# Attention and feed-forward in one block, narrow decode down products, and the last two groups finished row by row

## What is computed

```python
def hybrid_layer(x, ...):
    h = rmsnorm(x, norm_mix_pre)
    rq, rk, rv, rg, dq, dk, dv = split(h @ w_in)
    ret_out = silu(rg) * rms_normalize(retention(rope(rq), rope(rk), rv))
    diff_out = rms_normalize(diff_attention(rope(dq), rope(dk), dv))
    x = x + rmsnorm(concat(ret_out, diff_out) @ w_out, norm_mix_post)
    u = rmsnorm(x, norm_ffn_pre) @ w_up
    f = square(relu(u)) @ w_down
    return x + rmsnorm(f, norm_ffn_post)
```

## Time and profile before

| | us |
|---|---|
| median of 3 runs | 3050.96 (3050.58 to 3054.31) |
| the profiled execution | 3052.13 |
| its span, first to last instruction | 3050.3 |
| PE busy | 2894.8 |
| DVE busy | 1497.1 |
| ACT busy | 927.0 |
| POOL busy | 286.8 |

### The profile page before, as it was taken

The page is one execution under the profiler, slowest core; times in us unless marked ns, Lnnn a source line. Parts: engine busy times, 40 slices in busy tenths (PEclk is TensorE's granted clock), DMA queues, the critical chain, the costliest instruction groups (busy, mean ns, idle before and its releaser), DMA issues.

```text
span 3050.3 us, 39356 instructions
## 1 busy us (share of the span) xinstructions
PE 2894.8 (95%) x14977; PEld 2383.3 (78%) x14977; DVE 1497.1 (49%) x3014; ACT 927.0 (30%) x1852; POOL 286.8 (9%) x420
## 2 busy tenths in 40 slices
PE   6999997999969999999699999999989999999996
PEld 5888885778857777777478888888878989899895
DVE  4332233333247877777444444444565444544446
ACT  3222223222136666666321211121142112121112
POOL 1111220111111111100000000000021000000003
PEclk9999998999979999999799999999999999999998
DMA  4101103333332211110411111111042111111112
GB/s 161 34 27 32 35 21 130 126 100 124 125 124 83 68 65 56 39 43 29 147 60 42 54 42 51 46 41 55 28 141 96 42 41 41 45 51 41 41 55 100
DMA packets 105888, 204.68 MB, mean 67 GB/s; under 512 B 11248, under 2 KB 48112, under 8 KB 105776
## 3 DMA queue, kind: packets, MB, share of 16 engines
q1 hardware_dynamic: 103472, 194.79, 19.4%
q0 software_dynamic: 2304, 8.39, 0.8%
HBM read 168.28 MB, written 34.87 MB: 67 GB/s over the span
## 4 chain that ended last, share of the span: by engine, by line
PE 48%; DVE 2%; DMA 0%; ACT 0%; issue 0%; SPq 0%
PE bank L2135 24%; PE bank L2099 24%; DVE ffn_facc L1933 1%; PE bank L2090 0%; DVE ffn_upl L1907 0%; DVE ffn_facc L1974 0%; DVE ffn_hTl L1926 0%; DVE ffn_x L1920 0%; DMA ffn_gain_x<-in_norm_ffn_pre_dram 0%; DMA ffn_raw<-in_w_up_dram 0%; DVE ffn_dnl L1914 0%; DMA ffn_x<-x_scratch 0%; ACT ffn_hTh L1796 0%; ACT ffn_relu L1816 0%; DVE ffn_facc L1940 0%
## 5 line engine op out<-in xcount | busy, mean ns | idle before, releaser
L1974 DVE TENSOR_TENSOR ffn_facc<-bank,ffn_facc 128x512 f32<-128x512 f32 x510 | 345.9, 688 | 243.8 <-PE bank L2135 242.6
L2099 PE MATMUL bank<-ffn_hTh,ffn_uph 128*128 128x352 f32 (+1 forms) x1280 | 451.0, 352 | 8.7 <-DVE ffn_upl L1907 5.5
L2099 PE MATMUL bank<-ffn_hTl,ffn_uph 128*128 128x352 f32 (+1 forms) x1280 | 449.6, 351 | 0.0
L2099 PE MATMUL bank<-ffn_hTh,ffn_upl 128*128 128x352 f32 (+1 forms) x1280 | 449.4, 351 | 0.0
L2135 PE MATMUL bank<-ffn_dnh,ffn_hidh 128*128 128x512 f32 x1088 | 430.6, 396 | 9.4 <-DVE ffn_dnl L1914 6.2
L2135 PE MATMUL bank<-ffn_dnh,ffn_hidl 128*128 128x512 f32 x1088 | 430.7, 396 | 0.0
L2135 PE MATMUL bank<-ffn_dnl,ffn_hidh 128*128 128x512 f32 x1088 | 429.8, 395 | 0.0
L1947 DVE SCALAR_TENSOR_TENSOR ffn_relu<-bank,ffn_relu 128x352 f32<-128x352 f32 (+1 forms) x160 | 94.5, 591 | 482.2 <-ACT ffn_relu L1816 482.0
L2099 PEld LDWEIGHTS bank<-ffn_hTh,ffn_uph 128*128 128x128 f32 x1280 | 241.1, 188 | 33.7 <-issue 7.7
L2099 PEld LDWEIGHTS bank<-ffn_hTl,ffn_uph 128*128 128x128 f32 x1280 | 241.3, 188 | 23.6
L2099 PEld LDWEIGHTS bank<-ffn_hTh,ffn_upl 128*128 128x128 f32 x1280 | 241.1, 188 | 22.6
(11 more groups left out here) (196 smaller groups left out, 4393.3 us busy)
## 6 DMA issues: line engine op xcount, KB each, us to landing
ffn_raw<-in_w_up_dram SPq DMA_DIRECT2D x64, 512.0 KB, 4.5
ffn_raw<-in_w_down_dram SPq DMA_DIRECT2D x64, 512.0 KB, 4.1
ffn_x<-x_scratch SPq DMA_DIRECT2D x24, 512.0 KB, 4.1
retp_x<-in_x_prompt_dram SPq DMA_DIRECT2D x16, 512.0 KB, 3.6
retw_raw<-in_w_in_dram SPq DMA_DIRECT2D x16, 512.0 KB, 5.0
dpp_x<-in_x_prompt_dram SPq DMA_DIRECT2D x16, 512.0 KB, 5.0
dp_kst<-in_cache_diff_k_dram SPq DMA_DIRECT2D x32, 256.0 KB, 2.8
mix_xr<-in_x_prompt_dram SPq DMA_DIRECT2D x16, 512.0 KB, 3.4
```

The lines of the kernel that those rows point to most:

```text
L1974: nc.vector.tensor_tensor(out=part, in0=Dn[i % s.rd][:], in1=part, op=ALU.add).then_inc(s_add, 1)
L2099: last = nc.tensor.matmul(bank[:, 0:w], l[:, k, f * P:(f + 1) * P], r[:, k, c:c + w], start=(k == 0 and q == 0), stop=(k == 7 and q == 2))
```

## The change

Retention start: ACT takes the mean square of row tile 1 after eight of the 16 weight pieces. The constants are loaded between and behind the weight pieces: the small table behind piece 7, decay behind piece 11, the second rope table and the decode state behind piece 15.

Joined stages: attention and feed-forward are one phase, without a barrier between them. The programs of the attention are generators that yield at named points, and the feed-forward's programs run their first steps there. The feed-forward's buffers take the place of those of the attention that are free by then. On DVE the split of the last mixed rows now comes before the normalisation of tile 15.

Narrow decode products: ACT keeps a fp32 copy of the 32 decode columns of each hidden unit (`hd`). `decode_down` multiplies it with the unrounded weights in `raw`, as four fp32 matmuls with a 128x32 stationary tile, each into its own 32 rows of the bank `DD`, summed there over all 16 groups. `decode_sum` adds the two partial sums of each half with a matrix `pick`. The second block then has 96 matmuls per group and four banks in turn instead of three.

Last two groups: their second products are taken together, 12 matmuls into one bank, with the weights of the last group in the buffers of the up weights, and one accumulation for both. POOL makes only the inverse roots there; DVE multiplies with the gain while the root is made and finishes a row with one instruction. All residual rows have buffers of their own, seven of them loaded ahead.

```diff
                 wt.load(sp, wv, 0, slice(0, 4))
                 sp.dma_start(rope[0][:], rv[0][:, 0:192]).then_inc(s_rope[0], 16)
                 pre.load(sp, xv[1], 1)
-                sp.dma_start(rope[1][:], rv[1][:, 0:192]).then_inc(s_rope[1], 16)
-                sp.dma_start(decay[:], ret_tab[:, 0:4 * P]).then_inc(s_const, 16)
+                wt.load(sp, wv, 0, slice(4, 8))
                 sp.dma_start(small[:], ret_tab[:, 4 * P:4 * P + 12]).then_inc(s_const, 16)
+                wt.load(sp, wv, 0, slice(8, 12))
+                sp.dma_start(decay[:], ret_tab[:, 0:4 * P]).then_inc(s_const, 16)
+                wt.load(sp, wv, 0, slice(12, 16))
+                sp.dma_start(rope[1][:], rv[1][:, 0:192]).then_inc(s_rope[1], 16)
                 sp.dma_start(state[1][:].rearrange("d (h v) -> d h v", h=4),
                              state_in.rearrange("h d v -> d h v")).then_inc(s_const, 16)
-                wt.load(sp, wv, 0, slice(4, None))
...
-                wt.act_hi(act)
+                wt.act_hi(act, slice(0, 8))
+                pre.act_meansq(act, 1, 1, 2)
+                wt.act_hi(act, slice(8, 16))
...
+        def decode_down(g, e):
+            count = 2 * G + 2 * g + 3 - (1 if isinstance(g, int) and g == G - 1 else 0)
+            pe.wait_ge(s_hd, FG * (g + 1))
+            for i in range(FG):
+                pe.wait_ge(s_raw[i], 16 * count)
+            for n in range(2):
+                for f in range(FG):
+                    rows_out = slice((FG * n + f) * dec, (FG * n + f + 1) * dec)
+                    last = nc.tensor.matmul(DD[rows_out, :], hd[e][:, f, :], raw[f][:, n * N:(n + 1) * N],
+                                            start=(isinstance(g, int) and g == 0),
+                                            stop=(isinstance(g, int) and g == G - 1))
+            last.then_inc(s_dq, 1)
...
+        def down_both(s):
...
+            for i in range(s.rd):
+                half(i, 0)
+            decode_down(G - 1, 1)
+            pe.wait_ge(s_wlo, 8 * G)
+            pe.wait_ge(s_hl, s.u0 + G * s.ku)
+            for i in range(s.rd):
+                half(i, 1).then_inc(s_d, 1)
+            for i in range(s.rd, s.kd):
+                pe.wait_ge(s_add, 4 + d0 + i + 1 - s.rd)
+                half(i, 0)
+                if i == s.rd:
+                    decode_sum()
+                half(i, 1).then_inc(s_d, 1)
...
+                next(mixing)
+                pe.wait_ge(before_it.s_sc, before_it.read_pairs)
+                x_transpose(0)
+                x_transpose(1)
+                next(mixing)
+                x_transpose(2)
+                x_transpose(3)
+                next(mixing, None)
                 first_up(s, 0, range(0, 4))
...
+                if s.b and not last:
+                    sp.wait_ge(s_dq, g + 1)
...
                 hid_lo(s, 0, 0, 0, fu)
+                next(mixing, None)
...
                 x_lo(6)
...
+        for p, i in enumerate(s.order):
+            if i in s.whole:
+                accumulate(s, G - 2, i)
+            else:
+                decode_row()
+            if p:
+                last_row(p - 1)
+            gained(p)
+        last_row(s.nb - 1)
```

More of the change, by code:

```diff
@@ new lines, in mix_stage, with pair_banks, plan_transposes, bank_of @@
+    plan_pairs()
+    def pair_banks(u):
+        return SP_[2 * (u % 2)], SP_[2 * (u % 2) + 1]
+    t_use = {}
+    def plan_transposes():
+        i = itertools.count()
+        t_use["k", 0], t_use["q", 0] = next(i), next(i)
+        for n, (t, h) in enumerate(items):
+            for g in range(len(groups(t))):
+                t_use["A", n, g] = next(i)
+            if h == 0 and t + 1 < nt:
+                t_use["k", t + 1], t_use["q", t + 1] = next(i), next(i)
+    plan_transposes()
+    def bank_of(use):
+        return T[t_use[use] % 2]
@@ new lines, in ffn_stage, with loads, before, hid @@
+    slots.update({t: t % 2 for t in range(12, nt + 1)})
+    def loads(t):
+        return sum(slots[a] == slots[t] for a in range(t + 1))
+    def before(t):
+        return max((a for a in range(t) if slots[a] == slots[t]), default=None)
+    def hid(e, part):
+        return hidden_flat[e][part][:].rearrange("p (f n) -> p f n", f=FG)
+    class Shape:
+        def __init__(self, b):
+            self.b, self.tiles = b, blocks[b]
+            self.nb = len(self.tiles)
+            cols = sum(rows(t) for t in self.tiles)
+            w = cols // -(-cols // N)
+            self.subs = [(c, w) for c in range(0, cols, w)]
+            self.units = [(f, c, w) for f in range(FG) for c, w in self.subs]
+            self.first_units = [(f, c, w) for c, w in self.subs for f in range(FG)]
+            self.whole = [i for i in range(self.nb) if rows(self.tiles[i]) == P]
+            self.downs = [(i, n) for i in self.whole for n in range(2)]
+            self.order = self.whole[0:2] + [i for i in range(self.nb) if i not in self.whole] + self.whole[2:]
+            self.ku, self.kd = len(self.units), len(self.downs)
+            self.ru = 4 if self.ku % 4 == 0 else 3 if self.ku % 3 == 0 else 2
+            self.rd = 4 if self.kd % 4 == 0 else 3 if self.kd % 3 == 0 else 2
@@ new lines, in ffn_stage, with finished, residual @@
+    assert shapes[1].ru == 3 and shapes[1].rd == 4 and dec * 4 == P and G % 2 == 0
+    dnh2, dnl2 = (w[:].rearrange("p (f k) n -> p f (k n)", f=FG) for w in (uph, upl))
+    last_x = x + [gain_x] + raw + x[0:2]
+    def finished(b, p):
+        i = shapes[b].order[p]
+        t = blocks[b][i]
+        return i, t, shapes[b].t0 + p
+    def residual(eng, queue, p):
+        i, t, c = finished(0, p)
+        if p < 2:
+            eng.wait_ge(s_xT, 2 * (10 + p) + 2)
+        else:
+            eng.wait_ge(s_y, p - 1)
+        queue.dma_start(xe[p % 2][:], x1v[t]).then_inc(s_xe[p % 2], 16)
@@ L2188, in _ @@
-                down(s, G - 1, 1)
+                ffn.tensor(pe, mix.tensor(pe))
 def tables(seq, past, dec):
```

2195 lines of the change are left out of this document (1130 added, 1065 removed).

## The result

The changed kernel takes 2987.5 us at the median of four runs (2985.4 to 2989.0), the kernel before beside it 3051.6 us (four runs, 3050.6 to 3054.3): ratio 0.9785, 95% interval 0.9774 to 0.9797. It is faster by 64 us; 77 were forecast. The profiled execution of the changed kernel is the fastest of its four, 2985.4 us with a span of 2983.3, against 3050.3 before: 67.0 us in the spans.

A forecast was written before the change was run, and what follows sets the result against it. PE was taken as the bound, busy 2894.8 of 3050.3 us. The terms -28.3 - 21.4 - 24.0 - 3.5 = -77.2 us gave a forecast of 2974 us, range 2962 to 2991.

The forecast's parts named there:

- case (e): Whole kernel: the sizes of the prediction hold, 2974 us, own range 2964 to 2984; 71%.
- rival (b): Seam: it gives half, through slower transpose round trips and a lower clock; -12 us, 2986 us in all; 17%.
- a pack lasts over 1 us: Second block, packs of narrow decode products: a sign that the prediction is wrong; it put 0.7 us a pack.
- Narrow decode products: Second block: twelve matmuls fewer per group save 38.8 us, 15 packs of 0.7 us cost 10.5; net -28.3 us.
- The cross-check with the transposes: Decode scores: a transpose's 0.105 us gives 0.42 us for 512 fp32 columns, so four matmuls in 0.50 us run side by side.
- Rival (a): Packs: the four narrow matmuls run in turn, 2.2 instead of 0.7 us, 16 times; +24 us, 2998 us; 5%.
- The end: After the last first products: no wait for the last split, PE stays the bound; 75.8 us becomes 54.4, net -21.4.
- The seam: Between attention and feed-forward: first products start at 1482.3 instead of 1506.51 us; net -24.0, best -30, worst -12.
- The point that the split comes first: Seam, VectorE: the last mixed rows' split precedes normalising and adding the row before, ending at 1460.0 instead of 1462.65 us.
- the point on the last mixed row: Seam: its residual, square and root stand ahead of the rounding and split of feed-forward row 6; +2.6 us.
- (c): End: the last split isn't ready, or VectorE is still the bound and lags; +5 to +10 us, 2982 us; 5%.
- The start: Retention start: earlier square of row tile 1 lets PE go on at 43.7 instead of 47.21 us; net -3.5.

The follow-up runs named there:

- the second pack: In the changed kernel with every pack of narrow decode products made twice in a row, the repeat; that kernel took 3004.05 us.
- the experiment on VectorE's order: Changed kernel with normalisation and residual of mixed row 15 put ahead of the last mixed row's split again: 2987.3 us, 0.9785 of the kernel before.
- The control: The changed kernel run again unaltered beside other experiments: 2988.5 us, 0.9784 of the kernel before.

## Why the forecast came out as it did

The mechanisms are in the main as forecast, and each of the four steps gave less than its sum. The measured 2987.5 us lies within the whole range (2962 to 2991), but outside the range that case (e), with 71%, gave itself (2964 to 2984). It lies beside the 2986 us of rival (b), which didn't happen; that the two numbers meet is chance. One of the prediction's own signs of being wrong did come true: "a pack lasts over 1 us" (1.03 us for its products, 1.19 with the switches). The pack is the term that was mis-sized most.

**Narrow decode products (forecast -28.3, measured -22.6).** Removing twelve matmuls gave exactly the 2.77 us a group. The pack was mis-sized: 0.7 in the sum, 1.19 measured, 15 times 0.49 = 7.4 us too little; the 1.6 us between that and the 5.7 of the table come from places that I had not summed, the largest the second products of group 0 in block 2, which took 26.3 us before, 1.3 more than the others, and 23.25 with their pack now. The fault is in the reading of the earlier trace rows. A count behind a PE row counts records, and one plain fp32 matmul of the program leaves two. (Not every product is made of three fp32r matmuls, as the part on the kernel before has it: scores, weighted sums and the products of retention are plain fp32.) In the changed kernel it can be seen directly, since the last pack's four matmuls stand there as eight:

```profile
2932.29 0.40 PE L2242 MATMUL bank<-ffn_dnh,ffn_hidl 128*128 128x512 f32 x1
2932.62 1.06 PE L2271 MATMUL bank<-ffn_raw,ffn_hidden_decode 128*32 128x512 f32 x8
2933.61 0.50 PE L2242 MATMUL bank<-ffn_uph,ffn_hidh 128*128 128x512 f32 x1
```

So the eight of form 64*32 in the earlier trace rows were one pack in 1.00 us and not two in 0.50. The code would have told it: line 905 issues four products in a pack.

The cross-check with the transposes confirmed the wrong value for another reason. The transposes were counted rightly, since a transpose leaves one record. The prompt attention issues 544 weighted-sum matmuls and as many transposes of their weights (row tile j has j + 1 key blocks, 136 in all for 16 tiles, times 4 heads), and the kernel before shows them as

```profile
L1527 PE MATMUL bank<-mix_V,mix_AT 128*128 128x128 f32 x1088 | 140.4, 280 | 0.5 <-ACT mix_AT L1248 0.5
L1512 PE MATMUL bank<-kept_ident,mix_S 128*128 128x128 f32 x544 | 82.9, 280 | 26.4 <-DVE mix_S L1364 25.7
```

So the eight transposes in the earlier trace rows took 0.84/8 = 0.105 us each, as the prediction has it. But a transpose isn't the price of a matmul. Two pieces of weighted sums in the chain of the changed kernel, of nine and of ten matmuls:

```profile
1101.20 2.21 PE bank L1542 x18
1137.95 2.43 PE bank L1542 x20
```

One more matmul of 128 columns is 0.22 us, twice a transpose, and 512 columns are 0.88 us by it where the prediction had 0.42. The Trainium skill says of true fp32, in "FP8 and Floating Point Precision", section "TensorE Precision Notes", that it takes four passes through the array; the trace agrees: by an estimate from the 2.4 GHz of the granted clock 512 columns are 0.213 us a pass, and the second pack's 1.03 us is four of them and some overhead. Of the drain at a change of tiling mode (the Trainium skill, "TensorEngine Tiling (Array Packing)", "Tiling Modes") the runs now give the price, 0.16 us for both switches together; I had put 0.2. Rival (a), four in turn, would be 4 x 0.88 = 3.5 us, an estimate from the weighted sums, and is excluded. The waits of the pack cost nothing, as forecast: without packs the blocks touch, with them only the pack lies between.

**The end (forecast -21.4, measured -19.6).** The mechanism is as forecast: no wait for the last split, PE the bound up to the last bank, normalisations of 1.3 us in place of 2.73. Short by 1.8 us: PE's part took 47.1 us (2927.13 to 2974.2) instead of 46.4, most of it the mis-read pack, and 9.05 us instead of 8.0 lie behind the last matmul. The sum of the decode partials took 1.2 us as summed, but by luck: with two matmuls of 0.88 us one behind the other and the switch it would be about 2.0, an estimate, so the two must have overlapped; they stand on different halves of the rows. VectorE and POOL at the end:

```profile
2974.26 0.69 DVE L2058 TENSOR_TENSOR ffn_facc<-bank,ffn_facc 128x512 f32<-128x512 f32 x1 [1.87 <-PE bank L2242]
2974.87 1.27 DVE L2019 SCALAR_TENSOR_TENSOR ffn_facc<-ffn_facc,ffn_stats,ffn_x 128x1024 f32<-128x1024 f32 x1
2976.16 1.23 DVE L2010 TENSOR_TENSOR ffn_facc<-ffn_facc,ffn_gain_f 128x1024 f32<-128x1024 f32 x1
2977.89 1.28 DVE L2019 SCALAR_TENSOR_TENSOR ffn_facc<-ffn_facc,ffn_stats,ffn_x 128x1024 f32<-128x1024 f32 x1 [0.50 <-POOL ffn_stats L1812]
```

```profile
2976.44 1.35 POOL L1812 TENSOR_TENSOR ffn_stats<-ffn_stats,kept_rstd_x 128x1 f32<-128x1 f32 x1 [4.25 <-ACT ffn_stats L1865]
```

The four operations are each as summed, and the wait for the root is 0.50 us where 0.4 stood. POOL's root takes 1.35 us here, beside a product with two inputs from SBUF, and 0.55 us at 25.11 in the timeline of the start above, where VectorE ran an operation with one input from PSUM; VectorE waits 0.50 us for it. The Trainium skill, "GPSIMD Engine Reference", "1. Specifications", names a contention of POOL with VectorE instructions of two SBUF inputs; the gain product beside the root is one. No run took that product away from it, so this stays an attribution. What was short behind the last matmul is the issue and landing of the last store: 4.1 us from 2979.2 to 2983.3, where 3.0 was taken from the end before, whose last store is of 32 rows.

**The seam (forecast -24.0, measured -22.7).** First products at 1480.60, forecast 1482.3 less what the start gave (1.8), so 1480.5. The point that the split comes first is void, as the experiment on VectorE's order shows; the point on the last mixed row was under-priced, 3.7 and not 2.6. The first products of group 1, behind the wait of 5.46 us, ran partly at the lower level: 24.97 us at a granted clock of 0.89, against 23.96 at 0.93 before and 22.27 in the blocks behind. The rivals (b) and (c), both half-way losses, did not come: the first products start where the sum had them, and PE doesn't wait for the last split.

**The start (forecast -3.5, measured -3.3 at the first transposes, -1.8 at the seam).** It fits, and by the wrong comparison: in the changed kernel's first profile the gain vector landed 1.9 us earlier than in the profile before (VectorE's first product at 7.06 against 8.94), and I was ready to credit the new order with it. The control's profile has it at 8.97 and the first transposes at 45.42, so like with like it is -1.8 us. The landing differs by as much from run to run of the same code. And the step as a whole was asked too small a question: the wait for the state was in the sum as a bound of 40.0 us on POOL's work, but not what it meant, that the order costs 12 us, most of them through the semaphore that POOL shares with the state.

## What to carry to other kernels

Check a count in a profile row against the number of instructions in the source before dividing by it, and take the cross-check from the same kind of instruction: a transpose and a matmul of the same shape need not cost the same. When an engine waits for a semaphore that gathers several transfers, ask which of them the next operation reads: a bound on the last transfer is a cost, even where the sum comes out negative. A change in a queue's order should be priced alone, apart from the edits that come with it.

## What the runs showed of the hardware

A pack of four fp32 matmuls with 128x32 stationary tiles and 512 columns takes 1.03 us, about as long as one with 64x32 tiles (1.00); going to a narrower tile and back costs PE 0.16 us in all. A plain fp32 matmul leaves two records in the trace and costs 0.22 us for 128 columns, a transpose of a 128x128 fp32 tile leaves one and costs 0.105. A wait of 9.8 us on PE cost 2.2 us more through the granted clock (0.73 in the 8.5 us behind it), a wait of 1.51 us nothing (1.00). But a wait of 1.48 us with one of 2.33 and eight transposes ahead of it did cost: 0.88 over the 12.9 us behind it, 1.4 us. A root of 128 values on POOL took 0.55 us beside a VectorE operation with an input from PSUM, and 1.35 to 1.47 beside one with two inputs from SBUF. The first small loads of a program land up to 2.2 us apart from one execution to another (first transposes at 8.15 to 10.40 us in profiles of kernels whose first loads are the same).
